# Sixteen experts on one core: places without rows stand between used ones, four weight positions, and the second product one slot later

## The reference

```python
h = x + concat(o_attention, o_recurrence) @ w_out
xn = rms(h, norm2_w)
g = argmax(xn @ w_rg + b_rg)                      # one of 4 groups
top_v, top_i = top_k((xn @ w_re + b_re)[g], 2)    # 2 of its 4 experts
w_pair = softmax(top_v) * softmax(g_logit)[g]
y = h + sum over the 2 experts e of
        w_pair[e] * ((silu(xn @ w_gate[e]) * (xn @ w_up[e])) @ w_down[e])
```

## Time and profile before

| | us |
|---|---|
| median of 2 runs | 1463.34 (1461.02 to 1465.66) |
| profiled execution, its own time | 1457.58 |
| profiled execution, span | 1455.9 |
| PE busy | 1147.6 (79% of the span) |
| DVE, ACT, POOL busy | 574.3, 468.4, 248.6 |
| second product, gate and up product of the experts | 90.0 and 180.7 busy on PE |

### The profile page before, as it was taken

The page is one execution under the profiler, slowest core; times in us unless marked ns, Lnnn a source line. Parts: engine busy times, 40 slices in busy tenths (PEclk is TensorE's granted clock), DMA queues, the critical chain, the costliest instruction groups (busy, mean ns, idle before and its releaser), DMA issues. The chain is left out here.

```text
span 1455.9 us, 24335 instructions
## 1 busy us (share of the span) xinstructions
PE 1147.6 (79%) x9100; PEld 866.7 (60%) x9100; DVE 574.3 (39%) x1014; ACT 468.4 (32%) x885; POOL 248.6 (17%) x290
## 2 busy tenths in 40 slices
PE   4699999498988979168687875899929979999940
PEld 3699999386877868145465554777624434444410
DVE  5320120253636455677777873212151211222231
ACT  6111010245444454467667744212100101111121
POOL 4100000000000000332323222222010221222231
PEclk9999999799898989678888887999958999999975
DMA  4402310221212020699898974932223899997567
GB/s 126 116 23 67 88 31 0 60 75 46 88 45 88 30 85 20 215 347 321 290 315 284 311 237 164 312 121 102 66 69 119 235 272 280 283 288 234 141 148 193
DMA packets 161696, 230.55 MB, mean 158 GB/s; under 512 B 15921, under 2 KB 104498, under 8 KB 161522
## 3 DMA queue, kind: packets, MB, share of 16 engines
q1 hardware_dynamic: 144962, 174.20, 36.4%
q0 software_dynamic: 13568, 49.03, 13.0%
q10 hardware_dynamic: 3072, 6.03, 1.1%
HBM read 184.13 MB, written 49.55 MB: 161 GB/s over the span
## 5 line engine op out<-in xcount | busy, mean ns | idle before, releaser
L2171 PE MATMUL ps<-ring,e_xgT 128*128 x400 | 180.7, 606 | 11.3 <-SPq L2092 10.2
L2171 PEld LDWEIGHTS ps<-ring,e_xgT 128*128 128x128 f32 x400 | 75.8, 195 | 98.9 <-issue 98.9
L634 PE MATMUL ps<-xh,a_wh 128*128 128x384 f32 (+1 forms) x288 | 101.1, 351 | 0.0
L634 PE MATMUL ps<-xl,a_wh 128*128 128x384 f32 (+1 forms) x288 | 97.1, 337 | 0.0
L634 PE MATMUL ps<-xh,a_wl 128*128 128x384 f32 (+1 forms) x288 | 96.8, 336 | 0.0
L2123 POOL DMA_INDIRECT y_rows<-e_oE,slot_to x32 | 50.5, 1579 | 254.2 <-issue 203.5
L2203 PE MATMUL ps<-ring,e_hT 128*128 x200 | 90.0, 593 | 1.0 <-DVE e_oE L2272 1.0
L2265 DVE TENSOR_TENSOR e_hid<-e_sg,ps 128x256 f32<-128x256 f32 x32 | 13.4, 420 | 180.5 <-ACT e_sg L2230 180.5
L504 DVE COPY p_vs<-ps 128x256 f32<-128x256 f32 (+1 forms) x36 | 15.3, 424 | 172.7 <-PE ps L452 172.7
L452 PE MATMUL ps<-p_wvl,xh 128*128 128x256 f32 (+1 forms) x288 | 81.3, 282 | 0.0
L452 PE MATMUL ps<-p_wvh,xl 128*128 128x256 f32 (+1 forms) x288 | 81.3, 282 | 0.0
(11 more groups left out here) (352 smaller groups left out, 2431.2 us busy)
## 6 DMA issues: line engine op xcount, KB each, us to landing
d_K<-in_cache_k SPq DMA_DIRECT2D x128, 256.0 KB, 3.9
d_V<-in_cache_v SPq DMA_DIRECT2D x128, 256.0 KB, 5.2
ring<-in_w_gate SPq DMA_DIRECT2D x16, 1024.0 KB, 7.3
ring<-in_w_up SPq DMA_DIRECT2D x16, 1024.0 KB, 11.9
ring<-in_w_down SPq DMA_DIRECT2D x16, 1024.0 KB, 13.9
zT<-a_zs POOLq DMA_DIRECT2D x12, 544.0 KB, 3.0
a_w<-in_w_in SPq DMA_DIRECT2D x12, 512.0 KB, 3.8
y_rows<-ring SPq DMA_DIRECT2D x10, 512.0 KB, 2.6
```

The lines of the kernel that those rows point to most:

```text
L634: ins = pe.matmul(m.ps[:, 7, 0:w0], left[:, n % 2, k, :], right[:, k, c0:c0 + w0], start=(k == 0 and j == 0), stop=(k == KD - 1 and j == 2))
L2171: ins = pe.matmul(m.ps[:, 2 + u, :], xgT[:, u, k, :], up_k[:, bass.ds(r * KD + k, 1), :].squeeze(1), start=(k == 0), stop=(k == KD - 1))
```

## The change

1. **Order of the places.** Places without rows no longer stand together at the end. Every even place and the last one (31) are always used, which makes 17; an odd place i is used if used > 17 + i // 2. With `extra` = used - 17, the rank r (the place's number in the old list) goes to place r, or to 2 (r - extra) where that is more, at most 31 (`moved`, `poss`). For the inverse list, place i has rank min(i // 2, extra) + (i + 1) // 2 (`half`, `half_up`, `rank`).
2. **Four weight positions** (`RING` = 4, so `tile_ring` is `tile_expert & 3`). The third expert is loaded at the end of `mix_phase`, the fourth at the start of `moe_phase`. To make room, `mixA` and the second halves `row_of[1]`, `slot_of[1]` lie in ring memory; DVE waits for the stores of `hs` before it writes them.
3. **The second product one slot later.** PE, slot i: turn_x(i+1), up(i), turn_hidden(i-1), down(i-2). ACT and DVE follow: left(i-2), right(i-2). A skipped place waits for `hid_ready` and `ht_ready` before it counts its semaphores up.

```diff
-RING = 3
+RING = 4
+ALWAYS = TOP * TOK // 128
...
+                if t == NT - 1:
+                    sp.wait_ge(mix_split, 2 * TILES)
+                    load_expert(sp, a, m, 2)
...
+            do(dve.tensor_scalar(extra[:, :], cumf[:, NE - 1:NE], float(ALWAYS), None, ALU.subtract))
...
+            do(dve.tensor_scalar(moved[:, :, :], poss[:, :, :], extra[:, :], 2.0, ALU.subtract, ALU.mult))
+            do(dve.scalar_tensor_tensor(poss[:, :, :], moved[:, :, :], float(SLOTS - 1), poss[:, :, :], ALU.min, ALU.max))
 
             for j in range(TOP):
+                if j == 1:
+                    dve.wait_ge(hn_stored[0], 16 * (TILES // 2 + 1))
+                    dve.wait_ge(hn_stored[1], 16 * (TILES // 2))
...
-            load_expert(sp, a, m, 2)
-            landed(0)
-            landed(1)
-            landed(2)
+            load_expert(sp, a, m, 3)
+            for n in range(RING):
+                landed(n)
...
-                if i < ALWAYS:
+                if i % 2 == 0 or i == SLOTS - 1:
                     full()
                 else:
-                    with pe.If(used > i):
+                    with pe.If(used > ALWAYS + i // 2):
                         full()
...
                 def nothing():
+                    if i:
+                        pe.wait_ge(hid_ready, i)
                     pe.sem_inc(up_done, 1)
...
                 def unturned():
+                    if i:
+                        pe.wait_ge(ht_ready, i)
                     pe.sem_inc(h_turned, 1)
...
             for i in range(SLOTS):
                 if i + 1 < SLOTS:
                     turn_x(i + 1)
+                up(i)
                 if i:
                     turn_hidden(i - 1)
-                up(i)
-                if i:
-                    down(i - 1)
+                if i >= 2:
+                    down(i - 2)
             turn_hidden(SLOTS - 1)
+            down(SLOTS - 2)
             down(SLOTS - 1)
```

More of the change, by code:

```diff
@@ L147, in build @@
             m.cum = sb("cum", [1, NE], I32)
+            m.used = sb("used", [1, 1], I32)
             m.expert_in = [late.enter_context(nc.semaphore(f"expert_in{r}")) for r in range(RING)]
@@ L1697, in mix_phase @@
         mh, ml = sb("m_mh", [128, 2, KD, 128], F32R), sb("m_ml", [128, 2, KD, 128], F32R)
-        xT = m.ring[:, RING * UP + 2 * DOWN:RING * UP + 3 * DOWN].rearrange("p (u k n) -> p u k n", u=2, k=KD)
+        xT = m.ring[:, RING * UP + 3 * DOWN:RING * UP + 4 * DOWN].rearrange("p (u k n) -> p u k n", u=2, k=KD)
         wr = sb("m_wr", [128, KD, NR])
         br = sb("m_br", [128, NR])
-        xb = m.ring[:, 2 * UP:2 * UP + 2 * D].rearrange("p (u d) -> p u d", u=2)
-        hs = m.ring[:, 2 * UP + 2 * D:2 * UP + 4 * D].rearrange("p (u d) -> p u d", u=2)
+        xb = m.ring[:, 3 * UP:3 * UP + 2 * D].rearrange("p (u d) -> p u d", u=2)
+        hs = m.ring[:, 3 * UP + 2 * D:3 * UP + 4 * D].rearrange("p (u d) -> p u d", u=2)
         ss = sb("m_ss", [128, 2])
@@ L1717, in mix_phase @@
         someone = sb("m_someone", [128, SLOTS])
-        row_of = (xT[:, :, :, :].rearrange("p u k n -> p (u k) n")[:, 0:TILES, :], sb("m_row_of", [128, TILES, 128]))
+        row_of = (xT[:, :, :, :].rearrange("p u k n -> p (u k) n")[:, 0:TILES, :],
+                  hs[:, :, :].rearrange("p u (k n) -> p (u k) n", n=128)[:, 0:TILES, :])
         slot_of = (xT[:, :, :, :].rearrange("p u k n -> p (u k n)")[:, TILES * 128:TILES * (128 + 2 * SLOTS)].rearrange(
-            "p (t c s) -> p t c s", t=TILES, c=2), sb("m_slot_of", [128, TILES, 2, SLOTS]))
+            "p (t c s) -> p t c s", t=TILES, c=2), hs[:, :, :].rearrange("p u d -> p (u d)")[
+                :, TILES * 128:TILES * (128 + 2 * SLOTS)].rearrange("p (t c s) -> p t c s", t=TILES, c=2))
         posi, posr, poss = (sb(f"m_{n}", [128, TOP, TILES], I32) for n in ("posi", "posr", "poss"))
@@ L1726, in mix_phase @@
         posf = sb("m_posf", [128, 2, TILES])
-        tilef = sb("m_tilef", [1, SLOTS])
+        half = sb("m_half", [1, (SLOTS + 1) // 2, 2])
+        half_up = sb("m_half_up", [1, (SLOTS + 1) // 2, 2])
+        rank = sb("m_rank", [1, SLOTS])
+        extra = sb("m_extra", [128, 1])
+        moved = sb("m_moved", [128, TOP, TILES], I32)
+        last, twice = sb("m_last", [1, NE]), sb("m_twice", [1, NE])
         over = sb("m_over", [1, SLOTS, NE])
         ef = sb("m_ef", [1, SLOTS])
-        third = sb("m_third", [1, SLOTS], I32)
         wo_in = [sem(f"m_wo_in{c}") for c in range(WS)]
@@ L1734, in mix_phase @@
         gate = sem("m_gate")
-        mixA, mix_in = sb("m_mixA", [128, HEADS, SEQ]), [sem("m_mix_in0"), sem("m_mix_in1")]
+        mixA = m.ring[:, 2 * UP:3 * UP].rearrange("p (h n) -> p h n", h=HEADS)
+        mix_in = [sem("m_mix_in0"), sem("m_mix_in1")]
         w_rounded, w_split, mix_rounded, mix_split = (sem(f"m_{n}") for n in (
@@ L1834, in _ @@
                 do(pool.iota(value[:, j, :, 0], [[128, TILES]], base=1, channel_multiplier=1, allow_small_or_imprecise_dtypes=True))
-            do(pool.iota(tilef[:, :], [[1, SLOTS]], base=0, channel_multiplier=0, allow_small_or_imprecise_dtypes=True))
+            do(pool.iota(half[:, :, :], [[1, (SLOTS + 1) // 2], [0, 2]], base=0, channel_multiplier=0,
+                         allow_small_or_imprecise_dtypes=True))
+            do(pool.iota(half_up[:, :, :], [[1, (SLOTS + 1) // 2], [1, 2]], base=0, channel_multiplier=0,
+                         allow_small_or_imprecise_dtypes=True))
             for j in range(TOP):
@@ L1839, in _ @@
                 split_mix(t)
-        POOL_ALL = EG + 7 + 2 * TOP + 4 - 1
+        POOL_ALL = EG + 7 + 2 * TOP + 4
         @block.tensor
@@ L2041, in _ @@
                 dve.sem_inc(placed, 1)
-            do(dve.tensor_copy(m.cum[:, :], cumf[0:1, :]))
-            do(dve.tensor_tensor(over[:, :, :], tilef[:, :].unsqueeze(2).to_broadcast([1, SLOTS, NE]),
+            do(dve.tensor_copy(m.used[:, :], cumf[0:1, NE - 1:NE]))
+            do(dve.tensor_scalar(last[:, :], cumf[0:1, :], 1.0, None, ALU.subtract))
+            do(dve.tensor_scalar(twice[:, :], last[:, :], extra[0:1, :], 2.0, ALU.subtract, ALU.mult))
+            do(dve.tensor_tensor(last[:, :], last[:, :], twice[:, :], ALU.max))
+            do(dve.tensor_scalar(m.cum[:, :], last[:, :], 1.0, None, ALU.add))
+            do(dve.scalar_tensor_tensor(rank[:, :], half[:, :, :].rearrange("p k j -> p (k j)")[:, 0:SLOTS], extra[0:1, :],
+                                        half_up[:, :, :].rearrange("p k j -> p (k j)")[:, 0:SLOTS], ALU.min, ALU.add))
+            do(dve.tensor_tensor(over[:, :, :], rank[:, :].unsqueeze(2).to_broadcast([1, SLOTS, NE]),
                                  cumf[0:1, :].unsqueeze(1).to_broadcast([1, SLOTS, NE]), ALU.is_ge))
             do(dve.tensor_reduce(ef[:, :], over[:, :, :], AX.X, ALU.add))
[L2047 to L2052, removed]
+            do(dve.tensor_scalar(m.tile_expert[:, :], ef[:, :], float(NE - 1), None, ALU.min))
+            do(dve.tensor_scalar(m.tile_ring[:, :], m.tile_expert[:, :], RING - 1, None, ALU.bitwise_and))
             dve.wait_ge(listed, 1)
@@ L2066, in moe_phase @@
     XR = 4
-    ALWAYS = TOP * TOK // 128
     with ExitStack() as ctx:
@@ L2133, in _ @@
         def _(pe):
-            used = pe.value_load(m.cum[0:1, NE - 1:NE], min_val=0, max_val=SLOTS)
+            used = pe.value_load(m.used[0:1, 0:1], min_val=0, max_val=SLOTS)
             def turn_x(i):
@@ L2243, in _ @@
             for i in range(SLOTS):
+                silu(i)
                 if i:
                     hidden_out(i - 1)
-                silu(i)
-                if i:
-                    left(i - 1)
+                if i >= 2:
+                    left(i - 2)
             hidden_out(SLOTS - 1)
+            left(SLOTS - 2)
             left(SLOTS - 1)
@@ L2277, in _ @@
                 hidden(i)
-                if i:
-                    right(i - 1)
+                if i >= 2:
+                    right(i - 2)
+            right(SLOTS - 2)
             right(SLOTS - 1)
```

## The result

The changed kernel takes 1535.78 us (median of 2 runs, 1531.12 to 1540.44) where the kernel before takes 1463.34. The ratio is 1.0495, with a 95% interval of 1.0341 to 1.0650: slower by 72 us. The forecast was 1515 in a range of 1494 to 1540. The profiled execution took 1531.12 us with a span of 1529.2.

A forecast was written before the change was run, and what follows sets the result against it. PE bounds used places at 11.39 us each, with weight-load stalls and a POOL and DMA tail. Terms -32.3 (tail), +1 (drain), +84 (gaps), -1 (first places), +0.6 (lists) give +52 on 1463.3: 1515 us, range 1494 to 1540.

The forecast's parts named there:

- The mechanism: POOL's gather(j+5) waits behind scatter(j), now a slot later; PE stalls behind seven places without rows, 84 us lost.
- The tail: From last product to output copies: only one evacuation and scatter remain, 7.8 us instead of 40.1, 32.3 us gained.
- The lists: Three more small DVE steps ahead of the first half of the place lists: 0.6 us lost.
- The seven gaps: PE waits for gathers behind places without rows: six times 11.5 us, once 15.2, 84 us lost; bounds 72 to 101.
- the drain: PE's end of the expert loop: one more pair of products without cover, 1 us lost.
- The first of the seven gaps: At i = 16, slot 17 was given just 1.1 us of transposes to cover the gather.
- The clock: A product behind each gap starts at the lower clock level and lasts 7.93 us instead of 6.87, 1.06 us more.
- The first sixteen places: Weight waits fall from 14.6 to 7.3 us, gathers beside loads stall 7 us: 1 us gained in all.
- Hidden gathers: Rival: gathers are out early, so seven places without rows vanish beside products; about 1437 us, 4% chance.
- Half clock throughout: Rival: PE's clock does not come back within bursts, 9.3 us for each of seven, +65; 1580 us, 6% chance.
- Short waits: Rival: POOL runs ahead, so the seven waits average 8 us; +23, 1486 us, 6% chance.
- The scale: The sum on the profiled execution carried to the medians, which lie 5.8 us above: 1510 becomes 1515 us.

The follow-up runs named there:

- e2_ahead2: Changed kernel with POOL issuing the gather of place i+6, not i+4, ahead of scatter i; 1452.34 us, ratio to before 0.9922.
- e8_end_late_ahead2: Changed kernel with places without rows together at the end and gathers issued two turns earlier, second product still one slot later; 1455.30 us, ratio to before 0.9944.
- e4_at_end: Changed kernel with places without rows together at the end again, four positions and later second product kept; 1501.39 us, ratio to before 1.0274.
- e5_early_down: Changed kernel with the second product back in the next slot, alternation and four positions kept; 1447.52 us, ratio to before 0.9884.
- e3_up_all: Changed kernel with PE multiplying the gate and up product of places without rows as well; 1532.31 us, ratio to before 1.0479.
- e7_end_early_ahead2: Changed kernel with skipped places at the end, second product in the next slot, gathers two turns earlier; 1447.78 us, ratio to before 0.9918.

## Why the prediction was right, step by step

- **The mechanism** was the one named: gather j+5 behind scatter j, whose product comes one slot later, with the wait ahead of the branch. e2_ahead2 moves only POOL's order and takes 83 us away, e8_end_late_ahead2 46 us from e4_at_end; e5_early_down moves only the product and takes 88 us; e3_up_all shows that each gap holds 7 us of PE work for nothing.
- **The tail**: 32.3 us forecast, 32.6 measured.
- **The lists**: 0.6 forecast, 0.7 measured. The other 1.8 us of later start lie ahead of them and are not traced to the change.
- **The seven gaps**: 84 us forecast, about 99 measured together with the drain, for which 1 was forecast. This is the term that was too small, by 14 us. Its parts: the gather's issue 3.54 forecast, 3.44 measured; from landing to product 1.9 and 1.9 (1372.11 to 1374.05); the landing 6.1 forecast, 7.0 to 7.4 measured in the later pairs; the clock 1.06 forecast, 1.9 to 3.3 measured. I had kept the landing near because the next scatter would come 2.5 us behind the gather. It came 1.3 us behind (1366.12 after 1364.83), just as in the tail before, whose 7.59 of the earlier trace rows was the nearer row. And the first two gaps had gathers of 11.6 and 10.9 us beside weight loads, where I had one, at 9.8. (The fastest gather in the loop of before took 5.9 us; 6.0 was the fastest of those in the earlier trace rows.)
- **The first of the seven gaps** came out near its forecast by luck: its mechanism was another. I gave slot 17 only 1.1 us of transposes, but `down(15)` lies in it too, and place 15 is used. The gather of the skipped place 19, issued at 1310.44, landed after 8.8 us, before that product ended at 1321.06, and cost nothing. PE had waited 4.6 us before, for the gather of the used place 18, and ran `down(15)` slowly behind it, in 5.72 us instead of 3.43:

```profile
1311.56 1.97 PE L2164 MATMUL ps<-ident,e_xg 128*128 128x128 f32 x8 [4.56 <-DMA e_xg<-hn_rows,slot_from]
1314.30 0.66 PE L2208 MATMUL ps<-ident,e_hid 128*128 128x128 f32 x2 [0.78 <-issue]
1315.34 5.72 PE L2228 MATMUL ps<-ring,e_hT 128*128 x8 [0.38 <-issue]
```

- **The clock**: I took one product behind an idle PE, 7.93 us. The products behind the gaps took 8.8 to 10.1. In windows of 2 us their clock starts at 0.50, the lower of the two levels (1.2 GHz), and comes back at different points: the product of 1374.05 has the full clock from 1378 us on and takes 8.82 us, that of 1398.70 from 1406 on and takes 10.14. One row was too few for a cost that varies this much.
- **The first sixteen places**: 1 us gained forecast; lost were 5.0 - 0.5 = 4.5. Here the split was wrong, and the mis-sized term is the weights'. I forecast 7.3 us of weight waits for the late product. That is what the early product has (7.5 in e5_early_down); with the late one e2_ahead2 and e8_end_late_ahead2 lose 15.8 and 15.7, with no gather in the way. I had walked the three loads as 43.6 us; in e2_ahead2 they take 48.1 from the first issue (1162.64) to the last landing (1210.78), and I had put the slower products behind the waits at nothing. Of the changed kernel's 19.6 us of stall between silu 4 and silu 15, 13.9 lie at places 5 to 9. Waits for gathers and for weights are mixed there and hide each other, so no run parts them. The other 5.7 lie at places 11 to 15, where no weights are waited for. What I had missed there: when a gather lands just in time, PE's sequencer has no lead, and the reads ahead of `up` lie bare. Each place from 11 to 15 has such a row, at 0.4 to 0.9 us, place 12 for one:

```profile
1245.95 1.09 PE L2164 MATMUL ps<-ident,e_xg 128*128 128x128 f32 x8
1247.74 7.13 PE L2192 MATMUL ps<-ring,e_xgT 128*128 x16 [0.70 <-issue]
```

- **The rivals.** Hidden gathers (1437) fell; even with gathers two turns ahead the time is 1452. Half clock throughout (1580) fell: the windows named under the clock show it back at 1.00 within the product. Short waits (1486) fell too: six of the seven waits are 9.5 to 14.4 us long.
- **The scale**: the profiled execution lies 4.7 us below the median of the two runs after, 5.8 below that of before, so carrying the sum over to the medians was sound.

In sum, the miss of 21 us is 14 us of gaps, 5 of first places and 2 of a later start. The mechanism and the tail were right; the weights' term and the first gap were not, and they did little harm to the sum.

## What to carry to other kernels

When a step is moved one slot later, follow each queue that waits for it and ask what stands behind the waiting instruction: here it was not the scatter that hurt but the gather queued behind it. Work that is skipped by a branch still costs its waits, its transfers and the sequencer's reads, so mixing it among used work pays only if these are hidden better than at the end: in e5_early_down seven skipped places cost 4.4 us each among used ones, and at the end it would be 4.7 each (33 us for seven). And test a change's parts apart: four weight positions alone give about 12 us (8 to 17), and the change as a whole hides it under a loss of 72.

## What the runs showed that I had not expected

- A gather of 512 KB took 6.1 us where the next scatter came well behind it, 7.0 to 7.4 us with a scatter issued 1.3 us behind, and 10.9 to 11.6 us beside weight loads.
- Behind 3.2 us of idling PE's clock was mostly at the lower level in the product that followed (0.59 and 0.56 in two windows, 8.82 us instead of 6.87), yet another product of e2_ahead2 behind the same idling took 7.13. In e3_up_all, of three products behind gaps of 3.3 to 4.5 us one took 7.13 and one 10.05. The clock's loss is not a fixed price per gap.
- Silu 4 to silu 15 took 146.8 and 144.9 us in two kernels whose code is the same there but for the branches, and 150.1 in a third, which differs only in skipped places. Each is one profiled execution, and no run shows how far this stretch moves between executions of one kernel; so a difference of some us in it between two kernels should not be explained. That holds for e7_end_early_ahead2 too, whose profiled execution, the fastest of its six, is the only one with no wait for weights.
